# 64 free bytes in front of the transposed activations of a three-block transformer kernel

## What is computed

```python
def swiglu(x, w_in, w_out):
    a, b = jnp.split(x @ w_in, 2, axis=-1)
    return (jax.nn.silu(a) * b) @ w_out          # 1024 -> 2*2816 -> 1024

for l in range(DEPTH):                           # first block, DEPTH 1
    x = x + 0.5 * swiglu(rms_norm(x, ffn1_norm[l]), ffn1_w_in[l], ffn1_w_out[l])
    u = rms_norm(x, mix_norm[l]) @ w_in[l]
    ...
    x = x + mixed @ w_out[l]
    x = x + 0.5 * swiglu(rms_norm(x, ffn2_norm[l]), ffn2_w_in[l], ffn2_w_out[l])
for l in range(DEPTH_2):                         # second block, DEPTH_2 2
    x = x + 0.5 * rms_norm_2(swiglu_2(h, ffn1_w_in[l], ffn1_w_out[l]), ffn1_norm_post[l])
    ...
```

## Time and profile before

| | |
|---|---|
| time, median of 3 runs | 1866.52 us (1865.7 to 1870.53) |
| time of the profiled execution | 1861.96 us |
| its span, first to last instruction | 1860.2 us |
| TensorE matmul busy | 1832.6 us, 99% |
| TensorE weight load busy | 1678.5 us, 90% |
| VectorE busy | 1059.7 us, 57% |
| ScalarE busy | 918.9 us, 49% |
| GpSimd busy | 45.2 us, 2% |
| DMA | 329.19 MB, mean 177 GB/s |

### The profile page before, as it was taken

How to read it: one execution, slowest core, us unless ns; L and a number is a source line. 1 busy time by engine, 2 the same in 40 slices (tenths; PEclk the granted TensorE clock), 3 DMA queues, 4 the chain that set the end, 5 groups by cost and what they waited for, 6 DMA issues and landing times.

```text
span 1860.2 us, 33328 instructions
## 1 busy us (share of the span) xinstructions
PE 1832.6 (99%) x13114; PEld 1678.5 (90%) x13114; DVE 1059.7 (57%) x1413; ACT 918.9 (49%) x1200; POOL 45.2 (2%) x66
## 2 busy tenths in 40 slices
PE   8999999999999999999999999999999999999998
PEld 8999877999999999898898999899999887889997
DVE  5544777554555455655576544555474655575554
ACT  5344566434444445576555444444454675645343
POOL 0000220000000000000000000000000000000000
PEclk9999999999999999999999999999999999999999
DMA  8555423655465555452254554555555442345552
GB/s 313 196 182 194 178 92 114 222 184 203 167 238 201 186 176 204 165 198 92 91 180 176 200 184 173 207 205 200 187 186 192 159 161 93 134 170 200 184 196 97
DMA packets 47856, 329.19 MB, mean 177 GB/s; under 512 B 5392, under 2 KB 5648, under 8 KB 9616
## 3 DMA queue, kind: packets, MB, share of 16 engines
q1 hardware_dynamic: 44496, 316.84, 47.4%
q10 hardware_dynamic: 3264, 11.03, 1.8%
HBM read 326.80 MB, written 1.05 MB: 176 GB/s over the span
## 4 chain that ended last, share of the span: by engine, by line
issue 82%; PE 14%; POOL 1%; DVE 1%; ACT 1%; DMA 0%; DVEq 0%; POOLq 0%; ACTq 0%
PE work L1477 3%; PE work L1479 3%; PE work L1478 3%; POOL rstd L539 1%; PE acc L1477 1%; PE acc L1478 1%; PE acc L1479 1%; DVE lo L987 0%; DMA pre<-pre 0%; PE acc L1674 0%; PE acc L1570 0%; ACT hi L588 0%; PE acc L1694 0%; ACT squared L608 0%; PE acc L1683 0%
## 5 line engine op out<-in xcount | busy, mean ns | idle before, releaser
L987 DVE TENSOR_TENSOR lo<-raw,hi 128x2048 fp32r<-128x2048 f32 x280 | 640.3, 2291 | 476.8 <-ACT hi L588 476.5
L1477 PE MATMUL work<-xT_hi,hi 128*128 128x256 f32 x2752 | 770.8, 280 | 1.4 <-DVE lo L987 1.1
L1479 PE MATMUL work<-xT_hi,lo 128*128 128x256 f32 x2752 | 763.6, 277 | 0.0
L1478 PE MATMUL work<-xT_lo,hi 128*128 128x256 f32 x2752 | 763.6, 277 | 0.0
L588 ACT ACTIVATE hi<-raw 128x2048 fp32r<-128x2048 f32 x280 | 534.0, 1911 | 233.9 <-PE work L1479 188.1
L1477 PEld LDWEIGHTS work<-xT_hi,hi 128*128 128x128 f32 x2752 | 516.9, 188 | 17.9 <-issue 12.0
L1478 PEld LDWEIGHTS work<-xT_lo,hi 128*128 128x128 f32 x2752 | 517.0, 188 | 2.5
L1479 PEld LDWEIGHTS work<-xT_hi,lo 128*128 128x128 f32 x2752 | 518.9, 189 | 0.0
L1479 PE MATMUL acc<-hi,hT_lo 128*128 128x512 f32 x480 | 188.7, 393 | 0.0
L1478 PE MATMUL acc<-lo,hT_hi 128*128 128x512 f32 x480 | 188.2, 392 | 0.0
L1477 PE MATMUL acc<-hi,hT_hi 128*128 128x512 f32 x480 | 187.1, 390 | 0.0
(11 more groups left out here) (261 smaller groups left out, 2016.0 us busy)
## 6 DMA issues: line engine op xcount, KB each, us to landing
raw<-stream SPq DMA_DIRECT2D x298, 1024.0 KB, 4.8
pre<-pre ACTq DMA_DIRECT2D x7, 512.0 KB, 5.7
mem_in<-mem ACTq DMA_DIRECT2D x3, 1024.0 KB, 6.1
post<-post ACTq DMA_DIRECT2D x6, 512.0 KB, 3.8
x<-x SPq DMA_DIRECT2D x2, 512.0 KB, 4.9
pre<-pre SPq DMA_DIRECT2D x2, 512.0 KB, 3.5
out<-x SPq DMA_DIRECT2D x4, 256.0 KB, 2.0
alibi<-alibi ACTq DMA_DIRECT2D x1, 768.0 KB, 14.4
```

The source lines that it names most:

```text
L987: nc.vector.tensor_tensor(lo[:, s, :], raw[:, s, :], hi[:, s, :].bitcast(F32), ALU.subtract).then_inc(lo_ready, 1)
L1477: nc.tensor.matmul(dst, a_hi, b_hi, start=start, stop=False)
L1478: nc.tensor.matmul(dst, a_hi, b_lo, start=False, stop=False)
L1479: return nc.tensor.matmul(dst, a_lo, b_hi, start=False, stop=stop)
```

## The change

One call of `room` is added between `params` and `xT_hi`. Its result isn't used. `xT_hi` and everything behind it start 64 bytes later in each partition; `raw`, `hi`, `lo`, `x`, `xs`, `heads1`, `rot` and `params` stay. The distance of 192 (by 512) from the ring becomes 256. No instruction, wait, shape or transfer is added or removed.

```diff
         params = new("params", [P, max(B1P_N, LP_N)])
+        room(64)
         xT_hi = new("xT_hi", [P, KD, T], F32R)
         xT_lo = new("xT_lo", [P, KD, T], F32R)
         pre = new("pre", [P, D])
```

## The result

The changed kernel takes 1907.07 us (1905.78 to 1909.23, 4 runs), the kernel before 1866.11 us (1861.15 to 1870.53, 4 runs). The ratio is 1.0224, 95% interval 1.02 to 1.0247: it is slower by 2.2%, where I had forecast 0.6% faster. The profiled execution took 1907.4 us and its span is 1905.6 us, 45.4 us more than before.

A forecast was written before the change was run, and what follows sets the result against it. TensorE, 99% busy, was taken as the bound: number of matmuls times their step. With -12 us for channel products and nothing for the row form or other engines, 1866.5 - 12 = 1854.5 us, range 1838 to 1888.

The forecast's parts named there:

- The value taken for the channel part (-12 us): Products moving 256 activation columns against ring weights: 2750 slow ones settle, 4.4 ns less each, -12 us; chance 0.42.
- half a period apart: Moving and stationary operand, at distance 256 of a 512-byte period, are as far apart as possible, so more entries should settle.
- The upper end (+35 us): Worst bound: 6750 settled channel products turn slow, +30 us, and the row form adds 5 us.
- third gait: A TensorE matmul step slower than 117.7 ns, outside all rows; named as something that would make the prediction wrong outright.
- the settled one: The faster of two steady channel matmul steps, 113.3 ns, seen in the first block's second feed-forward; share 0.71.
- the slow one: The slower of two steady channel matmul steps, 117.7 ns, seen in the first block's first feed-forward; share 0.29.
- The row form: Matmuls moving 512 ring columns, some 2300, step 228.8 ns; lower end -8.5 us, upper end +5 us, nothing taken.
- The floor: Channel matmul step: neither another distance nor a shorter load had shown one under 113.3 ns.
- No cost on the other engines: ScalarE and VectorE use other addresses behind the gap, but their waits would cover even a tenth more; nothing taken.
- The control: Pairs wholly before or behind the gap keep their distance and cost nothing; the gates' products stay at 277 to 278 ns.
- Without effect: Rival: entry into a stretch sets the gait, addresses have no part; 1866.5 us, give or take 5; chance 0.27.
- The shift unsettles what is settled: Rival: 192 is the good distance; settled feed-forward loops turn slow, 4.4 ns per channel product, 1881 to 1901 us; chance 0.31.

The follow-up runs named there:

- m1: Matmul streams alone, without the transformer, at sixteen operand distances in two passes; channel step 120.0 ns at 0 and 256, 117.8 at 192.
- m3: `m2` with 64 distances in steps of 4 bytes and five entries each; 120.0, 113.3 and 121.7 ns at 108, 112 and 116.
- m2: Matmul streams alone, sixteen distances by 16 bytes, channel form entered nine times at each; 113.3 or 117.8 ns at 192, 120.0 at 0.
- e_ht_only: Changed kernel with the 64-byte gap moved from before `xT_hi` to before `r_qT`, so `xT` stays at 192; 1884.78 us beside 1866.03 of the kernel before.

## Why the prediction was wrong

*What bounds the kernel* was right: the number of matmuls times their step. Nothing that waits or moves data came near; with turns 0.58 us longer in five loops and 0.16 in one, the others only waited more.

*The value taken for the channel part (-12 us) failed*, and the step that failed is "at 256 both are half a period apart". I took the 512 of the ring's and the tiles' strides for the period of the hardware. It is 256 (`m1`: 0 and 256 agree, and so do the other seven pairs), so the change didn't take the operands farthest apart but put them at the same place, where every channel stretch went to 120.0 ns: about +48 us where I had -12. The argument behind it, that a greater distance settles more, fell as well: the true half, 128, has 118.3 to 120.0, and `m3` shows no slope from near to far at all. Even with the right period it would have pointed at a bad distance.

*The upper end (+35 us) was too small.* It let no channel product go beyond 117.7, as no row had more. The third gait is 120.0 ns: 6.7 ns more than the settled one, where the bound had 4.4, and 2.3 ns more than the slow one, where it had nothing. With these the same sum gives 6750 x 6.7 + 2750 x 2.3 = +52 us. The products with `cmp` at 116.9 I called nearest to an average over distances and then used as a price. They walk through good and bad distances, and load 30 columns; an average says nothing about the worst fixed distance. The bound should have been open upward. I had named a third gait only among the things that would make me wrong, and given it neither a price nor a chance.

*The row form* I took at 0 with -8.5 us as its end. It gained 2.1 ns x 2300 = 5 us by its regular steps, 3 us with the irregular ones behind each entry: inside the bounds. I had forecast no gain, so neither its sign nor its size was foretold.

*The floor* of 113.3 ns held in everything that ran: no distance of 64 goes under it.

*No cost on the other engines* held: busy times as before. The control held too: the gates at 278, `cmp` unchanged.

*The rivals.* "Without effect" fell with `m1`. Its rule, which the Trainium skill gives in "SBUF — State Buffer", section "Who interferes with whom", is that the moving operand and the weight loads have ports that are independent. The measurement decides otherwise for these fp32r streams: with only TensorE at work, 120.0 ns at distance 0 and 116.7 at 32. That the two reads hinder each other is the likely reading; what the runs show is the dependence on their distance. What was right in this rival is the part that the entry plays: it picks among the gaits that a distance offers (`m2`), and `e_ht_only` shows it in the kernel, where a change to the row form alone turned all channel loops slow. "The shift unsettles what is settled" had sign, place and cause right; its price of 4.4 ns ended at 1901 us, and the 6.7 ns that it should have had weren't in any row of before.

*Left open.* Why 112 and 192, and at some entries 16 and 144, reach 113.3, and why 113.3 is the floor, no run tells. Nor is it known what of the entry decides: one matmul more ahead changes it, its width alone doesn't settle it (`m2` against `m3`), and the time that passes and where the stream stands then are not told apart. Which of the two reads is held up isn't shown either; the weight loads of 192 ns at distance 0 are a hint for one distance only. Distances finer than 4 bytes, and tiles with other strides, weren't tried.

## What to carry to other kernels

When TensorE is 99% busy at its higher clock, read the distance between starts in several stretches of the same code: two values there mean that the operands' layout or the entry decides, and a bound taken from the gaits that one layout shows is no bound for another. Don't reason about which distance is good; measure it with a stream of matmuls alone, by the start addresses of the two operands counted by 256 bytes and with several entries, each long enough for its irregular first steps to pass (up to fifteen here), and fix the tile where the worst entry is fast. Measure again after anything is put ahead of it, since 64 bytes cost 2.2% here.

## What the runs showed of the hardware

- The step of fp32r matmuls depends on the distance between the start of the moving and that of the stationary operand in a partition, with period 256 bytes: from 113.3 to 123.3 ns for 256 columns, from 226.7 to 243.3 ns for 512.
- The dependence is as fine as 4 bytes: 120.0, 113.3 and 121.7 ns at 108, 112 and 116.
- At some distances the stream has two or more steps, each steady once entered (113.3 or 117.8 at 192), and what runs just ahead of it changes which. At 112 every entry seen ended at 113.3, after up to fifteen irregular steps.
- Channel and row form want different distances: 0 is 120.0 ns for the one, slower than most, and 226.7 for the other, its best.
- The gait of one stream can be set by the one before it: with the row form at 0, all loops at 192 took the slow one (16.75 us a turn, not 16.40 with 228.8 ns in the row form), at 112 none did (16.39).
